# Attention value products moved one step earlier on TensorE, behind the transposes of that step, in a hybrid encoder layer on one core

## What is computed

```python
qa = _rope_partial(_rmsnorm(q_a...), cos, sin); ka = the same of k_a
for window, dil in ((128, 1), (512, 4), (2048, 16)):
    scores = where(valid, einsum(q, k) * hd ** -0.5, NEG)
    p = exp(scores - max); l = sum(p)
    o = einsum(p, v) / l;  lse = max + log(l)
attn = sum over the patterns of softmax(lse)[i] * o_i, times silu(z_a)
y = concatenate([attn, hm]);  out = x + einsum(y, w_out)
```

## Time and profile before

| | |
|---|---|
| median of 3 runs | 2150.01 us (2148.2 to 2152.46) |
| the profiled execution | 2148.27 us |
| its span, first to last instruction | 2146.1 us |
| PE busy | 2068.2 us, 96% of the span |
| DVE busy | 1292.6 us, 60% |
| ACT busy | 846.7 us, 39% |
| mean granted TensorE clock | 0.977 of full speed |
| chain that ended last | PE 87%, DVE 4%, ACT 4%, issue 3% |

### The profile page before, as it was taken

The page is one execution under the profiler, slowest core; times in us unless marked ns, Lnnn a source line. Parts: engine busy times, 40 slices in busy tenths (PEclk is TensorE's granted clock), DMA queues, the critical chain, the costliest instruction groups (busy, mean ns, idle before and its releaser), DMA issues.

```text
span 2146.1 us, 27457 instructions
## 1 busy us (share of the span) xinstructions
PE 2068.2 (96%) x9536; PEld 1699.7 (79%) x9536; DVE 1292.6 (60%) x2670; ACT 846.7 (39%) x1350; POOL 174.0 (8%) x156
## 2 busy tenths in 40 slices
PE   5999999999999999999999999999998999999999
PEld 3887887888888888888878878778786877878887
DVE  7777758677677667767686646464565434343222
ACT  5553325344344335335453344352536343342110
POOL 4340000110110110010001101000010000000000
PEclk9999999999999999999999999999999999999999
DMA  4552344652562553463436535253344514235443
GB/s 161 181 162 79 113 139 141 142 133 79 142 148 84 132 130 108 119 146 99 137 133 163 112 67 130 57 115 84 89 99 142 192 53 149 77 113 183 147 140 111
DMA packets 140104, 264.62 MB, mean 123 GB/s; under 512 B 16320, under 2 KB 20928, under 8 KB 139712
## 3 DMA queue, kind: packets, MB, share of 16 engines
q1 hardware_dynamic: 121536, 229.32, 32.5%
q0 software_dynamic: 18432, 33.56, 11.1%
HBM read 168.44 MB, written 92.27 MB: 121 GB/s over the span
## 4 chain that ended last, share of the span: by engine, by line
PE 87%; DVE 4%; ACT 4%; issue 3%; DMA 1%; SPq 1%; DVEq 0%; ACTq 0%
PE ps L671 18%; PE ps L675 17%; PE ps L673 17%; PE ps L699 5%; PE ps L701 5%; PE ps L700 5%; PE ps L824 3%; PE ps L895 2%; PE ps L864 2%; PE ps L781 1%; PE ps L790 1%; PE ps L705 1%; PE ps L881 1%; PE ps L784 1%; PE ps L899 1%
## 5 line engine op out<-in xcount | busy, mean ns | idle before, releaser
L671 PE MATMUL ps<-t_hi,w_hi 128*128 128x512 f32 x1792 | 722.3, 403 | 40.4 <-DVE t_lo L1610 12.6
L675 PE MATMUL ps<-t_hi,w_lo 128*128 128x512 f32 x1792 | 705.6, 394 | 0.0
L673 PE MATMUL ps<-t_lo,w_hi 128*128 128x512 f32 x1792 | 705.5, 394 | 0.0
L671 PEld LDWEIGHTS ps<-t_hi,w_hi 128*128 128x128 f32 x1792 | 341.3, 190 | 115.6 <-issue 49.7
L675 PEld LDWEIGHTS ps<-t_hi,w_lo 128*128 128x128 f32 x1792 | 341.0, 190 | 73.9
L673 PEld LDWEIGHTS ps<-t_lo,w_hi 128*128 128x128 f32 x1792 | 342.0, 191 | 66.4
L933 ACT CAST w_hi<-w_raw 128x512 fp32r<-128x512 f32 x256 | 158.5, 619 | 427.7 <-PE ps L701 214.5
L1158 DVE TENSOR_TENSOR w_lo<-s_tmp,w_hi 128x512 fp32r<-128x512 f32 x256 | 182.2, 712 | 135.0 <-ACT w_hi L933 125.7
L933 ACT CAST w_hi<-s_tmp 128x512 fp32r<-128x512 f32 x256 | 158.6, 620 | 258.8 <-PE ps L675 239.2
L1158 DVE TENSOR_TENSOR w_lo<-w_raw,w_hi 128x512 fp32r<-128x512 f32 x256 | 182.1, 711 | 124.3 <-ACT w_hi L933 117.5
L699 PE MATMUL ps<-t_hi,w_hi 128*128 128x512 f32 x384 | 157.0, 409 | 0.7 <-DVE xt L1601 0.7
(11 more groups left out here) (216 smaller groups left out, 2858.0 us busy)
## 6 DMA issues: line engine op xcount, KB each, us to landing
w_raw<-w_all_dram SPq DMA_DIRECT2D x320, 256.0 KB, 3.5
fin_dram<-xt SPq DMA_DIRECT2D x128, 256.0 KB, 4.0
fin_dram<-xt POOLq DMA_DIRECT2D x128, 256.0 KB, 4.3
arena<-fin_dram SPq DMA_DIRECT2D x64, 512.0 KB, 5.1
arena<-xT_dram SPq DMA_DIRECT2D x48, 256.0 KB, 6.3
arena<-xT_dram SPq DMA_DIRECT2D x16, 512.0 KB, 3.8
y_raw<-y_dram SPq DMA_DIRECT2D x16, 512.0 KB, 5.0
s_tmp<-xT_dram SPq DMA_DIRECT2D x32, 256.0 KB, 4.0
```

The costliest lines, as they stand in the source:

```text
L671: nc.tensor.matmul(ps[:, bank, :], hi, t_hi[:, n, k, :], start=new and k == 0, stop=False, skip_group_check=True)
L673: nc.tensor.matmul(ps[:, bank, :], hi, t_lo[:, n, k, :], start=False, stop=False, skip_group_check=True)
L675: mm = nc.tensor.matmul(ps[:, bank, :], lo, t_hi[:, n, k, :], start=False, stop=k == KP - 1, skip_group_check=True)
```

## The change

`values(j)` moves from step 15 + 2j to step 14 + 2j on PE, and within the step from before `prob_transposes` to behind it. The multiplication of its result with the gate on DVE (L1569) moves from step 16 + 2j to 15 + 2j, and the store of the head's result on SP (L521) from step 23 to 22. No instruction is added or removed, and no wait condition is changed.

```diff
@@ attention_loads (SP)
-                if at == 23:
+                if at == 22:
                     sp.wait_ge(a_y, 4 * h + 4)
                     sp.dma_start(y_dram[ATT_HEADS + h], ystage).then_inc(a_out, 16)
@@ attention_pe
                 if at == 11:
                     value_transposes(h)
-                if at in (15, 17, 19, 21):
-                    values(h, (at - 15) // 2)
                 if 0 <= at - 12 < 8:
                     prob_transposes(h, at - 12)
+                if at in (14, 16, 18, 20):
+                    values(h, (at - 14) // 2)
@@ attention_dve
-                if at in (16, 18, 20, 22):
-                    j = (at - 16) // 2
+                if at in (15, 17, 19, 21):
+                    j = (at - 15) // 2
```

## The result

The changed kernel takes 2112.59 us (median of 4 runs, 2112.39 to 2113.87) against 2151.17 us (2148.2 to 2152.46) for the kernel before: a ratio of 0.9824, 95% interval 0.9807 to 0.9841. That is 38.6 us less. The profiled executions, to which the working of the prediction belongs, differ by 2148.27 - 2112.56 = 35.7 us, and their spans (2146.1 and 2110.4) by the same.

The account below looks back on a forecast made before the run. PE was taken as the bound, busy 2068 of 2146 us. Savings of 20.0 - 0.5 + 9.0 + 3.2 = 31.7 us, less 1.7 for small new waits, gave 2150 - 30 = 2120 us, range 2110 to 2133.

Parts of the forecast that it names:

- rival 4: Whole kernel: more goes than counted, the clock falls luckily and head 4 loses its wait, 30 + 5 + 3: 2112 us; chance 0.04.
- deduction of 1.7: Taken off the summed saving for small new waits, such as one in head 5 at DVE's output addition: 1.7 us.
- The price of a place, 0.87 us: Transposes (L881) waiting for ACT's copy, steps 15, 17, 19: 4.34 - 2.89 - 0.58 = 0.87 us saved each, 23 places, 20.0 us.
- The larger figure of 1.02: Same places: if no gap stayed between values and product, each would save 1.02 us, 23.5 in all; not adopted.
- The six waits for DVE follow from the stall, 9.0 us: Step 18, heads 0 to 5: transposes' waits for DVE's copy go, since DVE's queue only started late; 9.0 us saved.
- Three of the six waits of the scores, 3.2 us: Scores (L864), head 2 step 16, head 4 steps 16 and 17: waits for DVE's masking go, 3.2 us saved.
- Head 4: nothing saved, 0.5 lost, a wait of 2.6: Head 4, steps 18 to 19: ACT's 8.9 us chain stays, so a 2.6 us wait stays; 0.5 us lost.
- The clock, counted at nothing between 5 gained and 4 lost: Low clock behind each head's square sums: the change shifts the stretches, 5 us gained to 4 lost; taken as nothing.
- rival 3: DVE, moved gate product: y waits for the values and delays work behind it, making scores late; 2166 us, chance 0.03.
- The store on SP costs nothing, and an earlier one only helps DVE, off the path: SP, heads 3, 5, 6: store ahead of loads and an output store costs nothing; gate's buffer freed sooner only helps DVE.

Follow-up runs that it names:

- j = 0: Kernel before with only each head's first values moved to step 14 behind the transposes, their gate product to step 15: 2138.37 us, ratio 0.9945.
- j = 2: Kernel before with only each head's third values moved to step 18 behind the transposes, their gate product to step 19: 2141.94 us, ratio 0.996.
- j = 1: Kernel before with only each head's second values moved to step 16 behind the transposes, their gate product to step 17: 2132.37 us, ratio 0.9914.
- j = 3: Kernel before with only each head's fourth values moved to step 20, gate product to step 21, store to step 22: 2146.77 us, ratio 0.9989.

## Why the prediction was right, point by point

The forecast was 2120 us, range 2110 to 2133; the time is 2112.59, in the range near its lower end. That is also the number of rival 4 (2112: 30 us, 5 of clock, 3 of head 4), which had a chance of 0.04. The mechanism forecast is the one that the traces show, but not all that brought the time so low was foreseen. Between the profiled executions 35.7 us went, not 30: the clock added 4.7, as rival 4 says, and the deduction of 1.7 did not come, while the start took 1.6 back. Head 4 kept its wait, against rival 4. The rest of the way to 38.6 is the reference, below.

- **The price of a place, 0.87 us.** Confirmed in its parts: 2.89 us for the values with a product behind them, measured 2.89; 0.58 for the transposes, measured 0.57 (1253.53 to 1254.10). The kernels with j = 0 and j = 2 alone, which hold 8 and 7 plain places, gave 9.5 and 5.9 us for 9 and 6. The larger figure of 1.02, by which the gap behind the values should vanish, did not come: from the first L899 to the product are 0.63 us in the changed kernel, as in the earlier trace rows.
- **The six waits for DVE follow from the stall, 9.0 us.** Confirmed by the kernel with j = 1 alone.
- **Three of the six waits of the scores, 3.2 us.** Confirmed: 5.0 us fell to 2.0, for a forecast of 2.3. The three that are left are the three named, in steps 11 and 14.
- **Head 4: nothing saved, 0.5 lost, a wait of 2.6.** Too dark. The wait is 1.76 us, and the transposes of steps 18 and 19 stand 8.3 us apart (1629.56 to 1637.88), not 8.9, against 8.2 before, so 0.15 us were lost. (By the prediction's own rows, 8.9 - 8.2, the loss would have been 0.7, not 0.5.) ACT's exponential of block 7 began 0.6 us before the transposes of step 18, not with them. Splitting the input one unit later shortened the wait as the chain said. The rows of the changed kernel:

```profile
1628.93 0.88 ACT L1063 ACTIVATE arena<-arena,mins 128x704 f32<-128x704 f32 x1
...
1629.56 0.60 PE L881 MATMUL ps<-ident,arena 128*128 128x128 f32 x4
...
1637.22 0.56 ACT L1076 COPY arena<-ps 128x512 f32<-128x512 f32 x1
...
1637.88 0.63 PE L881 MATMUL ps<-ident,arena 128*128 128x128 f32 x4 [1.76 <-ACT arena L1076]
```

- **A deduction of 1.7 us for small new waits.** None came; the list of waits has no new entry, and the 0.7 us in three waits for DVE's output addition (L699 for L1601) are gone from it.
- **The clock, counted at nothing between 5 gained and 4 lost.** This is the term that was mis-sized: between the profiled executions it gave 4.7 us. The reason given for zero, that the work ahead of the sums "has the same length apart from the wait that goes", put aside in half a sentence the wait with which, by the traces, the long stretches go. How much of the 4.7 us belongs to the change is not shown; part may be luck. Low clock past the square sums, us:

| values and wait ahead of the sums | | without them | |
|---|---|---|---|
| before | 38.8 | changed kernel | 29.5 |
| j = 0 | 34.2 | j = 2 | 32.4 |
| j = 1 | 35.9 | values ahead of the transposes | 33.5 |
| j = 3 | 40.3 | input split one unit later | 35.6 |
| | | gate product and store late | 36.7 |
| | | store late | 37.5 |

The means are 37.3 and 34.2 us; half the difference is 1.6 us. The changed kernel's trace is the lowest of its group, and the kernel before lies above its group's mean.
- **A slip in rival 3.** The work that ends at 6.1 us less the copy of 0.43 ends at 5.7, not 5.9. It changes nothing in the verdict.
- **The store on SP costs nothing, and an earlier one only helps DVE, off the path.** Right in its first half, wrong in its second. With PE's own waits gone and the store late, DVE's wait behind the small transfers is on the path, 1.3 to 3.75 us in head 4. I had looked for what the store stands ahead of and not for what it would stand right behind if it had not moved.

The sum of the prediction's terms, 31.7, with 4.7 for the clock and -1.6 for the start, is 34.8 of the 35.7 us between the profiled executions; the smaller loss in head 4 and the waits for L1601 cover most of the difference. The other 2.9 us of the 38.6 are how far the profiled execution of before lay below its median (2148.27 against 2151.17); in the later comparisons the median of the kernel before was 2147.86 to 2149.57.

## What to carry to other kernels

When a wait closes on itself (the producer that holds the buffer is just ahead, on the same engine, of the instruction that needs it refilled), put a long independent piece of work between the two; the exact place within that piece does not matter. Look for the waits further on that are only the late start of a queue: here they were reckoned at 12 us, beside 20 for the direct ones. And thin work of PE is better spread between dense work than kept together or cut in two, but it must be spread far enough: here 16 sums in one product gained nothing, and 8 in each of two did.

## What the hardware showed that was not expected

- A 128x1 float32 matmul with its own 128x128 weights (two records) takes 0.46 us in a row of 16 of them, at either level of the clock, and 0.385 between 128x512 ones at the upper level.
- The low clock comes in stretches that outlast their cause: 7.4 us of such matmuls in one piece brought 6.8 or 10.2 us of it, and 13.6 or 13.7 twice in head 5, where PE had waited just before; two pieces of 3.7 us brought, in head 3, two stretches of 6.8 us each; the same work at two for every three 512-column matmuls over two products brought none.
- With the sums in one piece, heads 1 to 7 of ten kernels, the length of the stretch went with the moment of the fall: 10 us or more in all 36 cases where the clock fell no later than 3.33 us behind the start of the sums, 6.8 us in all 34 where it fell later. With values and an idle of 0.8 us just ahead 24 of 28 were long, in the other order 12 of 42.
- Between runs of one kernel the time goes with the mean clock: of the runs of the kernel before, those at a mean clock of 0.979 and 0.980 took 2144.56 to 2147.63 us, those at 0.974 and 0.975 took 2147.9 to 2153.22.
